# Samples' inputs and spread decays: the order of two TensorE blocks in a state-space stage

## The chip, the core and the metric

The kernel runs on one core of a Trainium2 chip. The metric is the device time of one execution in microseconds; the median of three runs of the kernel before is 1073.29 (1071.87 to 1075.68). TensorE does the matmuls and the transposes, VectorE and ScalarE the work between them, GpSimd issues the stores and SyncE most loads. Each engine runs its own list of instructions in order, and the lists meet at semaphores.

## What is computed

One inference step of two layers for a prompt of 256 tokens and for 8 samples with 4 new tokens each (32 sample tokens). Layer 0 is a short convolution beside block-sparse attention, layer 1 a Mamba-2 mixer, and each is followed by a SwiGLU network. The change lies in the mixer of layer 1, in the part for the samples. Cut to what matters there:

```
xbc = silu(causal_dwconv(xbc, conv_hist, conv_w) + conv_b)
xs, b_in, c_in = split(xbc)                    # 2048 inputs, 4 groups x 128 of B and of C
dt = softplus(dt + dt_bias);  a = -exp(a_log)
xdt = xs * dt
a_cum = cumsum(dt * a)
chunk_states = einsum('bclgn,bclgr,bclgrp->bcgrpn', b_in, exp(a_cum[-1] - a_cum), xdt)
state = state * exp(a_cum[-1]) + chunk_states  # one state of 32 heads x 64 x 128 a sample
y_diag = einsum(C B^T, exp(a_cum[l] - a_cum[s]), xdt);  y_off = einsum(C, old state, exp(a_cum))
```

So each of the 8 samples' states (1 MB each) is loaded, multiplied by a decay for each head, added to a product of weighed inputs and B, and stored.

## The kernel before

Everything is float32. Activations stand with channels on the 128 partitions and the 288 tokens (256 prompt, 32 sample) along the row; `NP:NT` are the samples' columns. `XBC` holds the convolved channels: 16 tiles of inputs, then B and C. After the last projection of layer 1, TensorE's list is: turn the per-head quantities (L1272 to L1276, read by VectorE into `tc`) and B (L1278 to L1283), the products of C and B for four groups (L1284 to L1290), then the part that the change touches:

- Spreading the decays (L1296 to L1300): 32 heads, one small matmul each, which the trace shows as 64 instructions, nine columns wide: the eight samples' decays and the skip weight of each head, from `decin`, are put on the 64 partitions of the head. VectorE copies the result to `dec` (L2583).
- Turning the samples' inputs (L1301 to L1305): for each of `G` = 4 groups, `PG` = 4 transposes of 128x32 pieces of `XBC` into one bank, so that the 32 sample tokens stand on partitions.
- Spreading the samples' sums for the differences (L1306 to L1312): 2 banks of 16 heads each, 64 matmul instructions in the trace.

Then `turn_state(0, q)` turns the four quarters of sample 0's state (L1315 to L1326), and the loop over the samples runs (L1371 to L1379): `new_state` multiplies weighed inputs `XW3` by B for one quarter (L1328 to L1339), `turn_state` turns a quarter of the next sample's state, `from_state` multiplies the old state by C (L1341 to L1349).

What orders this work: there are four banks `acc`, used in turn. `acc_open()` on TensorE (L831 to L836) waits until the bank four uses back was given free, and VectorE's `take()` (L1935 to L1940) waits for the bank next in the same count. So VectorE must read the banks in the order in which TensorE fills them, and a swap on one engine needs the same swap on the other.

VectorE's list there: the masked products of C and B (L2578 to L2582), the copy to `dec` (L2583), then for each group two products of the turned inputs with per-head weights, `XWT` (L2602) and `XDS` (L2603), and one group later the rest `XW3` (L2595, `rest_x`). Then the differences are added into `SEGS` (L2609), cut at zero (L2612), and the states are updated, 16 instructions a sample (L2620), each with a column of `dec`. Before each `rest_x`, ScalarE rounds that group's inputs twice (L1854, L1855). After the fourth group it makes a mask (L1836, `mask_b(1)`) and only then copies the turned quarters of state 0 (L1846). The third `turn_state` waits for the first of these copies (L1322). After its four quarters, a state is stored by GpSimd (L802 to L805); five states lie in a ring of buffers from before, one in a buffer of its own, and the last two are loaded by SyncE (L622 to L634) when the stores of states 0 and 1 have landed.

Of the kernel before, what the change touches and what calls it, by code (L numbers as in the profile page):

```python
# [23 lines left out]
P = 128  # L24
# [3 lines left out]
def hybrid_decoder_kernel(  # L28
# [8 lines left out]
):  # L37

    _, NP, D = x_prompt.shape
    NB, T, _ = x_sample.shape  # L40
    NS = NB * T
    NT = NP + NS
# [13 lines left out]
    CX = DI // P  # L56
    NST = state_ssm.shape[3]
    CC = state_conv_ssm.shape[2] // P
    G = (CC - CX) // 2
    HG = SH // G  # L60
    PG = HG // 2
# [32 lines left out]

    HIST_POS = 4
    Z_UNITS = [pos for pos, (kind, _) in enumerate(IN1) if kind == "z"]
    in1_units = [x for kind, i in IN1 for x in column_units(l1_w_in, (DI if kind == "c" else 0) + i * UC, 1)]

# [16 lines left out]
    with ExitStack() as ctx:  # L115
        def sb(name, shape, dt=F32):
            return ctx.enter_context(nc.sbuf_tensor(name, shape, dt))

        def sem(name):
            return ctx.enter_context(nc.semaphore(name))  # L120
# [109 lines left out]
        XBC = a.take(CC, NT)  # L230
# [35 lines left out]
        ident = sb("ident", [P, P])  # L266
# [30 lines left out]
        dec = a.take(CX, NB + 1)  # L297
# [55 lines left out]
        acc_full = sem("acc_full")  # L353
# [158 lines left out]
        def acc_bank(n):  # L512
            return acc[(n if n < ACC_MIX else n + 2) % 4]
# [92 lines left out]
        for w in (l0_norm_mix_pre, l0_norm_mix_post, l0_norm_ffn_pre, l0_norm_ffn_post,  # L606
                  l1_norm_mix_pre, l1_norm_mix_post, l1_norm_ffn_pre, l1_norm_ffn_post, l1_norm_gate):
            k = w.shape[0] // P
# [77 lines left out]
        def _(pool):  # L686
# [95 lines left out]
            for i, (src, _) in enumerate(conv_units):  # L782
                if i:
                    pool.wait_ge(cw_lo, 2 * i)
                pool.dma_start(WST, src).then_inc(cw_in, 16)
# [39 lines left out]
        def _(pe):  # L825
# [5 lines left out]
            def acc_open():  # L831
                n = n_acc[0]
                n_acc[0] += 1
                if n >= 4:
                    pe.wait_ge(acc_free, n - 3)
                return acc_bank(n)  # L836

            def tr_open(n):
                if n >= 2:
                    pe.wait_ge(tr_act if n % 2 == 0 else tr_dve, n // 2)  # L840
                return trb[n % 2]
# [137 lines left out]
            for k in range(KD):  # L979
                bank = tr_open(TR_X + k)  # L980
                for t in range(3):
                    rows = P if t < 2 else NS
                    last = pe.transpose(bank[:, t * P:t * P + rows], XIN[0:rows, t, k * P:(k + 1) * P], ident[0:rows, 0:rows])
# [26 lines left out]
            for i, m in enumerate((MK, MV)):  # L1010
                for t in range(3):
                    rows = P if t < 2 else NS
                    bank = tr_open(TR_KV + 3 * i + t)
                    for c in range(H * DH // P):
                        last = pe.transpose(bank[0:rows, c * P:(c + 1) * P], BIG[:, m + c, t * P:t * P + rows], ident[:, :])
# [243 lines left out]
            bank = acc_open()  # L1259
            pe.wait_ge(wdt_lo, 2)  # L1260
            for k in range(KD):
# [3 lines left out]
                last = pe.matmul(bank[0:SH, 0:NT], low, HX1[:, k, 0, :], start=False, stop=(k == KD - 1))  # L1265
# [6 lines left out]
            bank = acc_open()  # L1272
            for t in range(3):
                rows = P if t < 2 else NS
                last = pe.transpose(bank[0:rows, t * P:(t + 1) * P], hs[:, t * P:t * P + rows], ident[:, :])
            last.then_inc(acc_full, 1)  # L1276
            pe.wait_ge(xc_made, 2 * CC)
            for t in range(3):  # L1278
                rows = P if t < 2 else NS
                bank = acc_open()  # L1280
                for g in range(G):
                    last = pe.transpose(bank[0:rows, g * NST:(g + 1) * NST], XBC[:, CX + g, t * P:t * P + rows], ident[:, :])
                last.then_inc(acc_full, 1)  # L1283
            for g in range(G):  # L1284
                bank = acc_open()
                for t in range(3):
                    rows = P if t < 2 else NS
                    cols = slice(t * P, t * P + rows)
                    last = pe.matmul(bank[0:rows, cols], XBC[:, CX + g, cols], XBC[:, CX + G + g, cols], start=True, stop=True)
                last.then_inc(acc_full, 1)  # L1290
            def spread_head(out, h, of_heads):

                half = slice(h % 2 * DH, (h % 2 + 1) * DH)
                return pe.matmul(out[half, :], ident[0:SH, h:h + 1].to_broadcast([SH, DH]), of_heads, start=True, stop=True)

            bank = acc_open()  # L1296
            for h in range(SH):
                k = h // 2
                last = spread_head(bank[:, k * (NB + 1):(k + 1) * (NB + 1)], h, decin[:, :])
            last.then_inc(acc_full, 1)  # L1300
            for g in range(G):  # L1301
                bank = acc_open()
                for c in range(PG):
                    last = pe.transpose(bank[0:NS, c * P:(c + 1) * P], XBC[:, g * PG + c, NP:NT], ident[:, :])
                last.then_inc(acc_full, 1)  # L1305
            for i in range(2):  # L1306
                bank = acc_open()
                for hh in range(SH // 2):
                    h = i * SH // 2 + hh
                    last = pe.matmul(bank[0:NS, hh * NS:(hh + 1) * NS], ident[0:SH, h:h + 1].to_broadcast([SH, NS]), hw[:, 0, NP:NT],  # L1310
                                     start=True, stop=True)
# [148 lines left out]
            for g in range(G):  # L1460
# [10 lines left out]
                for c in range(PG):  # L1471
                    bank = acc_open()
                    for r in range(2):
# [3 lines left out]
                        for t in range(2):  # L1477
                            pe.matmul(bank[rows, t * P:(t + 1) * P], XDT[:, gp, t, cols], SEG[gp][:, hh, t * P:(t + 1) * P],
                                      start=True, stop=(t == 0))
                        last = pe.matmul(bank[rows, P:2 * P], SENT[gp][:, cols], CE[gp][hh // 4][:, hh % 4 * P:(hh % 4 + 1) * P],  # L1480
                                         start=False, stop=True)
# [12 lines left out]
            for i in range(2):  # L1494
                pe.wait_ge(x_made, 3 * KD + 4 * i + 4)
                for t in range(3):
                    rows = P if t < 2 else NS
                    for c in range(4):
                        last = pe.transpose(Y_BANKS[3 * i + t][0:rows, c * P:(c + 1) * P], X[:, 4 * i + c, t * P:t * P + rows], ident[:, :])
# [432 lines left out]
        def _(dve):  # L1932
            n_acc, chain, n_r = [0], [0], [0]

            def take():  # L1935

                n = n_acc[0]
                n_acc[0] += 1
                dve.wait_ge(acc_full, n + 1)
                return acc_bank(n)  # L1940

            def free(ins):
                ins.then_inc(acc_free, 1)
# [74 lines left out]
            for i, m in enumerate(range(MQ, M_IN0)):  # L2018
                bank = take()
# [20 lines left out]
            for r in range(2):  # L2040
                rows = slice(r * DH, (r + 1) * DH)
                last = dve.tensor_copy(KNZ[rows, :, :].rearrange("p (c r) n -> p c r n", r=2)[:, :, r, :],
                                       BIG[rows, MK:MK + H // 2, NP:NT])
# [519 lines left out]
            bank = take()  # L2563
# [14 lines left out]
            for g in range(G):  # L2578
                bank = take()
                dve.tensor_tensor(CBM[:, g, 0:NP].rearrange("p (t c) -> p t c", c=P), bank[:, 0:NP].rearrange("p (t c) -> p t c", c=P),  # L2580
                                  trilT[:, :].unsqueeze(1).to_broadcast([P, 2, P]), ALU.mult)
                free(dve.tensor_tensor(CBM[0:NS, g, NP:NT], bank[0:NS, NP:NT], bd01[:, :], ALU.mult))  # L2582
            free(dve.tensor_copy(dec[:, :, :], take()[:, 0:CX * (NB + 1)].rearrange("p (k c) -> p k c", c=NB + 1)))  # L2583

            def by_head(rows, t, first, g):

# [5 lines left out]
            def rest_x(g):  # L2592
                cols = slice(g * HG * DH, (g + 1) * HG * DH)
                dve.wait_ge(xw_hi, 2 * g + 2)
                dve.tensor_tensor(XW3[2 * NS:S3, cols], XWT[g % 2][0:NS, :], XW3[0:NS, cols], ALU.subtract).then_inc(xw_lo, 1)  # L2595

            for g in range(G):
                bank = take()
# [5 lines left out]
                if g >= 1:  # L2604
                    rest_x(g - 1)
            rest_x(G - 1)
            for i in range(2):
                mine = slice(i * SH // 2, (i + 1) * SH // 2)
                free(dve.tensor_tensor(SEGS[0:NS, mine, :], take()[0:NS, :].rearrange("p (h n) -> p h n", n=NS),  # L2609
                                       tc[0:NS, 2, AC + i * SH // 2:AC + (i + 1) * SH // 2].unsqueeze(2).to_broadcast([NS, SH // 2, NS]), ALU.add))  # L2610
# [3 lines left out]
            for b in range(NB):  # L2614
                st = state_home(b)[0]
                for q in range(G):
                    bank = take()
                    for hh in range(PG):
                        k = q * PG + hh
                        last = dve.scalar_tensor_tensor(st[:, k, :], st[:, k, :], dec[:, k, b:b + 1],  # L2620
                                                        bank[:, hh * NST:(hh + 1) * NST], ALU.mult, ALU.add)
# [59 lines left out]
            for g in range(G):  # L2681
# [9 lines left out]
                for c in range(PG):  # L2691
                    k = g * PG + c
# [46 lines left out]
```

## Time and profile before

| | us |
|---|---|
| median of three runs | 1073.29 (1071.87 to 1075.68) |
| the profiled execution | 1074.21 |
| its span, first to last instruction | 1072.5 |
| TensorE busy with matmuls | 1022.2 (95%) |
| VectorE busy | 691.8 (65%) |
| ScalarE busy | 500.0 (47%) |

A busy time is a sum over the whole span; what a change in one stage can do is read from the order of events in that stage. The instruments are the chain of work that ended last, which follows from the end back to what released each step; the timeline of one engine, with the idle time before an instruction and its releaser; and the stretches, which give each engine's busy time and the clock granted to TensorE (1.00 is 2.4 GHz, 0.50 is 1.2 GHz). Times in the trace count from the start of the span.

### The profile page before, as it was taken

How to read it: one execution, taken by the hardware profiler on the slowest of the kernel's cores; microseconds unless marked ns; L12 is line 12 of the kernel's file. 1: busy time of each engine (PE TensorE's matmuls, PEld its weight loads, DVE VectorE, ACT ScalarE, POOL GpSimd, SP SyncE). 2: the span in 40 equal slices, each digit the busy share in tenths (PEclk: the TensorE clock that was granted, in tenths of full speed). 3: DMA queues.
4: the chain of work that ended last, by engine and by line, in shares of the span. 5: the costliest groups of instructions: out<-in, count | busy, mean ns of one | idle time of the engine just before them, and what ended most of it. 6: DMA issues, size and time to landing. Idle time of an engine off the chain costs nothing.

```text
span 1072.5 us, 22412 instructions
## 1 busy us (share of the span) xinstructions
PE 1022.2 (95%) x9097; PEld 941.6 (88%) x9097; DVE 691.8 (65%) x1284; ACT 500.0 (47%) x899; POOL 56.4 (5%) x106
## 2 busy tenths in 40 slices
PE   9999999997899999999999999899899899999996
PEld 8987886664789999999889999678789799999996
DVE  5556787544467656634588996788965766665343
ACT  5233453421454334434457764565754544444331
POOL 6050000000000000000000000021000000000000
PEclk8999999998899999999999999699999999999999
DMA  9859999999935555445335565098145255544501
GB/s 302 232 153 349 348 347 346 348 348 347 296 91 184 158 163 178 151 156 178 120 118 158 173 180 145 15 295 318 31 140 175 80 167 181 164 157 144 181 31 45
DMA packets 187782, 206.22 MB, mean 192 GB/s; under 512 B 7226, under 2 KB 178447, under 8 KB 187628
## 3 DMA queue, kind: packets, MB, share of 16 engines
q1 hardware_dynamic: 166222, 170.79, 50.6%
q0 software_dynamic: 5680, 18.79, 5.4%
q10 hardware_dynamic: 15776, 15.21, 4.5%
q8 instruction: 72, 1.18, 0.5%
q14 instruction: 32, 0.25, 0.1%
HBM read 192.59 MB, written 12.17 MB: 191 GB/s over the span
## 4 chain that ended last, share of the span: by engine, by line
PE 73%; DVE 9%; SPq 8%; DMA 5%; issue 2%; ACT 1%; ACTq 0%; POOL 0%; DVEq 0%
PE acc L935 20%; PE acc L937 20%; PE acc L936 19%; SPq L658 8%; DMA ring<-in_cache_k_dram 2%; PE scb L1180 2%; DVE X L2402 1%; DMA ring<-in_state_ssm_dram 1%; DVE Y L2399 1%; DVE HX L1979 1%; PE trb L1030 1%; PE acc L1163 1%; DMA ring<-in_cache_v_dram 1%; DMA out_dram<-ring 1%; PE scb L1051 1%
## 5 line engine op out<-in xcount | busy, mean ns | idle before, releaser
L935 PE MATMUL acc<-HX,WHL 128*128 128x288 f32 x800 | 238.2, 298 | 3.0 <-DVE HX L1977 1.3
L936 PE MATMUL acc<-HX,WHL 128*128 128x288 f32 x800 | 236.0, 295 | 0.0
L937 PE MATMUL acc<-HX,WHL 128*128 128x288 f32 x800 | 235.8, 295 | 0.0
L1545 ACT ACTIVATE WHL<-ring 128x1024 fp32r<-128x1024 f32 x126 | 124.7, 1038 | 165.5 <-PE acc L937 160.2
L1990 DVE TENSOR_TENSOR WHL<-ring,WHL 128x1024 fp32r<-128x1024 f32 x126 | 146.9, 1206 | 62.4 <-ACT WHL L1545 62.3
L935 PEld LDWEIGHTS acc<-HX,WHL 128*128 128x128 f32 x800 | 150.6, 188 | 4.8 <-DVE ext L2446 1.5
L936 PEld LDWEIGHTS acc<-HX,WHL 128*128 128x128 f32 x800 | 151.8, 190 | 0.0
L937 PEld LDWEIGHTS acc<-HX,WHL 128*128 128x128 f32 x800 | 151.6, 189 | 0.0
L1545 ACT ACTIVATE W<-ring 128x1024 fp32r<-128x1024 f32 x84 | 82.6, 1031 | 132.6 <-PE acc L937 129.9
L1990 DVE TENSOR_TENSOR W<-ring,W 128x1024 fp32r<-128x1024 f32 x84 | 97.1, 1197 | 52.8 <-ACT W L1545 52.7
L935 PE MATMUL acc<-HX,W 128*128 128x288 f32 x336 | 99.5, 296 | 0.2 <-DVE Z L2416 0.2
L936 PE MATMUL acc<-HX,W 128*128 128x288 f32 x336 | 98.8, 294 | 0.0
L937 PE MATMUL acc<-HX,W 128*128 128x288 f32 x336 | 98.7, 294 | 0.0
L936 PEld LDWEIGHTS acc<-HX,W 128*128 128x128 f32 x336 | 63.5, 189 | 0.0
L935 PEld LDWEIGHTS acc<-HX,W 128*128 128x128 f32 x336 | 63.0, 187 | 0.6 <-DVE Z L2416 0.4
L937 PEld LDWEIGHTS acc<-HX,W 128*128 128x128 f32 x336 | 63.4, 189 | 0.0
L935 PE MATMUL acc<-HID,W 128*128 128x288 f32 x176 | 52.1, 296 | 0.0
L935 PE MATMUL acc<-HID,WHL 128*128 128x288 f32 x176 | 52.1, 296 | 0.0
L936 PE MATMUL acc<-HID,WHL 128*128 128x288 f32 x176 | 51.7, 294 | 0.0
L936 PE MATMUL acc<-HID,W 128*128 128x288 f32 x176 | 51.7, 294 | 0.0
L937 PE MATMUL acc<-HID,W 128*128 128x288 f32 x176 | 51.7, 294 | 0.0
L937 PE MATMUL acc<-HID,WHL 128*128 128x288 f32 x176 | 51.7, 294 | 0.0
(447 smaller groups left out, 2053.6 us busy)
## 6 DMA issues: line engine op xcount, KB each, us to landing
ring<-in_l_w_in_dram SPq DMA_DIRECT2D x26, 1024.0 KB, 5.3
ring<-in_l_ffn_gate_dram SPq DMA_DIRECT2D x22, 1024.0 KB, 5.3
ring<-in_l_ffn_up_dram SPq DMA_DIRECT2D x22, 1024.0 KB, 5.3
ring<-in_cache_k_dram SPq DMA_DIRECT2D x83, 256.0 KB, 7.2
ring<-in_cache_v_dram SPq DMA_DIRECT2D x76, 256.0 KB, 7.8
ring<-in_l_ffn_down_dram SPq DMA_DIRECT2D x16, 1024.0 KB, 5.1
ring<-in_l_w_out_dram SPq DMA_DIRECT2D x11, 1024.0 KB, 9.7
ring<-in_cache_v_dram ACTq DMA_DIRECT2D x32, 256.0 KB, 7.5
```

The source lines that it names most:

```text
L658: sp.dma_start(dst, src).then_inc(landed, 16)
L935: pe.matmul(out, w[:, 0, at:at + P], part_at(k, 0), start=(k == 0), stop=False)
L936: pe.matmul(out, w[:, 0, at:at + P], part_at(k, 1), start=False, stop=False)
L937: last = pe.matmul(out, w[:, 1, at:at + P], part_at(k, 0), start=False, stop=(k == kdim - 1))
L1030: last = pe.transpose(TURNED[q][jp][:, hh * P:(hh + 1) * P], keys[:, 4 * q + hh, 2 * jp:2 * jp + 2, :].rearrange("p j d -> p (j d)"), iden ...
L1051: last = pe.matmul(scb[e][g * QT:(g + 1) * QT, s * P:(s + 1) * P], QZ[:, e, q, hh * QT:(hh + 1) * QT], KTB[p % 2][:, jp, q, hh * P:(hh + 1 ...
L1163: pe.matmul(bank[:, 0:NT], w[:, 0, at], HX0[:, k, 0, :], start=(k == 0), stop=False)
L1180: last = pe.matmul(bank[j * QT:(j + 1) * QT, :], S[:, b, s, j * QT:(j + 1) * QT], POOL[(N_SLOT + b * KVS + s) % NPL][:, :, j, :], start=(s ...
L1545: act.activation(split_weights(i)[:, 0, half], source[:, half], ACT.Copy).then_inc(w_hi, 1)
L1979: ins = dve.scalar_tensor_tensor(hx[:, k, 1, :], X[:, k, :], par[:, 0, col:col + 1], hx[:, k, 0, :], ALU.mult, ALU.subtract)
L1990: dve.tensor_tensor(w[:, 1, half], landing(i)[0][:, half], w[:, 0, half], ALU.subtract).then_inc(w_lo, 1)
L2399: link(dve.tensor_tensor(y, y, SPREAD_R.unsqueeze(1).to_broadcast([P, size, NT]), ALU.mult))
```

## The change

TensorE turns the samples' inputs first and spreads the decays after them. VectorE reads the banks in the new order: the copy to `dec` moves from ahead of the products of the inputs to behind the last of them and its rest, ahead of `SEGS`. No instruction is added, removed or altered.

```diff
@@ -1293,16 +1293,16 @@
+            for g in range(G):
+                bank = acc_open()
+                for c in range(PG):
+                    last = pe.transpose(bank[0:NS, c * P:(c + 1) * P], XBC[:, g * PG + c, NP:NT], ident[:, :])
+                last.then_inc(acc_full, 1)
             bank = acc_open()
             for h in range(SH):
                 k = h // 2
                 last = spread_head(bank[:, k * (NB + 1):(k + 1) * (NB + 1)], h, decin[:, :])
             last.then_inc(acc_full, 1)
-            for g in range(G):
-                bank = acc_open()
-                for c in range(PG):
-                    last = pe.transpose(bank[0:NS, c * P:(c + 1) * P], XBC[:, g * PG + c, NP:NT], ident[:, :])
-                last.then_inc(acc_full, 1)
@@ -2580,7 +2580,6 @@
-            free(dve.tensor_copy(dec[:, :, :], take()[:, 0:CX * (NB + 1)].rearrange("p (k c) -> p k c", c=NB + 1)))
@@ -2604,6 +2603,7 @@
                 if g >= 1:
                     rest_x(g - 1)
             rest_x(G - 1)
+            free(dve.tensor_copy(dec[:, :, :], take()[:, 0:CX * (NB + 1)].rearrange("p (k c) -> p k c", c=NB + 1)))
```

## Rows read from the trace of the kernel before

**Rows 1.** The page: granted clock in 40 slices, and the chain's shares by engine.

```profile
PEclk8999999998899999999999999699999999999999
...
PE 73%; DVE 9%; SPq 8%; DMA 5%; issue 2%; ACT 1%; ACTq 0%; POOL 0%; DVEq 0%
```

**Rows 2.** The chain that ended last, 672 to 722: start, duration, engine, tile, line.

```profile
672.17 3.34 PE acc L1294 x64
...
676.51 0.68 DVE hists L2602
...
683.92 0.72 ACT BM L1836
...
687.95 0.87 PE trb L1324 x4
...
693.28 2.17 DVE ring L2620 x8
...
701.86 7.38 DMA out_dram<-ring
...
709.30 12.00 DMA ring<-in_state_ssm_dram
...
721.35 0.66 PE trb L1324 x4
```

**Rows 3.** Timeline of TensorE: start, duration, instruction, count, idle before and releaser.

```profile
675.44 3.59 PE L1304 MATMUL acc<-ident,Z 128*32 128x128 f32 x16
678.96 2.35 PE L1310 MATMUL acc<-Z,ident 32*32 32x32 f32 x64
681.24 1.09 PE L1324 MATMUL trb<-ident,ring 128*128 128x128 f32 x8
685.26 1.94 PE L1324 MATMUL trb<-ident,ring 128*128 128x128 f32 x8 [2.93 <-ACT Z L1846]
```

**Rows 4.** Timeline of VectorE, 673 to 688.

```profile
673.23 0.17 DVE L2582 TENSOR_TENSOR Z<-acc,bd 32x32 f32<-32x32 f32 x1
675.55 0.31 DVE L2583 COPY late<-acc 128x144 f32<-128x144 f32 x1 [2.15 <-PE acc L1294]
...
682.50 0.67 DVE L2603 TENSOR_TENSOR Z<-acc,late 32x512 f32<-32x512 f32 x1
...
683.92 0.68 DVE L2595 TENSOR_TENSOR XW<-ext,XW 32x512 fp32r<-32x512 f32 x1
...
687.99 1.12 DVE L2620 SCALAR_TENSOR_TENSOR ring<-ring,late,acc 128x128 f32<-128x128 f32 x4 [1.36 <-PE acc L1337]
```

**Rows 5.** Stretches: length, busy by engine (count), granted clock, DMA share, GB/s.

```profile
672.60:675.40 2.80, 2.80 (x56) 2.80 (x54) 0.80 (x4) 0.00 (x0) 0.00 (x0) 0.50 0.01 4
675.50:678.90 3.40, 3.40 (x17) 2.16 (x16) 2.70 (x5) 1.63 (x3) 0.00 (x0) 0.50 0.00 0
679.50:681.20 1.70, 1.70 (x58) 1.70 (x54) 1.56 (x4) 1.65 (x4) 0.00 (x0) 1.00 0.05 14
...
685.30:689.50 4.20, 4.20 (x21) 4.20 (x22) 2.42 (x7) 3.13 (x5) 0.00 (x0) 0.50 0.00 0
689.60:692.80 3.20, 3.20 (x15) 1.21 (x14) 1.12 (x4) 1.56 (x3) 0.00 (x0) 0.50 0.00 0
...
700.00:720.00 20.00, 20.00 (x176) 15.93 (x175) 17.44 (x66) 13.65 (x25) 4.64 (x4) 1.00 0.93 292
```

**Rows 6.** The chain again, later, where the clock is granted in full.

```profile
722.40 0.46 PE trb L1324 x4
...
738.99 1.98 PE acc L1294 x64
```

**Rows 7.** Timeline of ScalarE: the third copy of a turned quarter.

```profile
686.39 0.60 ACT L1846 ACTIVATE Z<-trb 128x512 f32<-128x512 f32 x1 [0.79 <-PE trb L1324]
```

**Rows 8.** Timeline of GpSimd: the first store of a state.

```profile
696.36 1.21 POOL L768 DMA_DIRECT2D out_dram<-ring  x1 [28.61 <-DVEq L2624]
```

**Rows 9.** Waits of SyncE's queue, 690 to 760: total, times, longest.

```profile
SPq L634 <- DMA out_dram<-ring: 69.6, 7, 35.9
```

## The prediction

> **What bounds the kernel now.** I read the page first. The granted clock and the shares of the chain that ended last [rows 1] say that TensorE carries the program as a whole: 73% of the chain is its own work, and the rest is short stretches in which it waits for somebody. The change touches one of these stretches, some 20 us long, between the last projection of layer 1 and the recurrent states. So the question is which piece ends last there, and the chain of work in order of time answers it [rows 2]. Read it downward. From 672.17 the chain is TensorE spreading the decays (64 small matmuls, 3.34 us), then the first four transposes of the samples' inputs, and at 676.51 VectorE takes over with its weighing of these inputs. VectorE stays the chain until ScalarE rounds the last group and makes a mask (683.92, 0.72 us). ScalarE can copy the first turned state only then, at 684.64. TensorE, whose own list had been done long before, goes on at 685.26 [rows 3]. From there TensorE feeds VectorE, which updates states 0 and 1; the store of state 1 (7.38 us) and the load of the last state into the same buffer (12.00 us) bring the chain to 721.35.
>
> The timeline of each engine says who waits. On TensorE [rows 3] the spread, the transposes, the samples' differences and two turned states follow each other without a hole from 672.17 to 682.33, and then it waits 2.93 us for ScalarE's copy. On VectorE [rows 4] the last masked product starts at 673.23 and takes 0.17; then VectorE waits 2.15 us for the spread, copies it in 0.31, waits again (0.65 us) for the first transposes, and has no hole more until its first state update at 687.99, before which it waits 1.36 us.
>
> **The change, part by part.** It adds and removes nothing. It swaps two blocks in TensorE's list and moves one VectorE copy behind the eight products and four remainders of the inputs. No DMA is issued in the moved pieces and no other engine's list changes, so SyncE's and GpSimd's queues are passed by nothing.
>
> (1) TensorE starts the transposes at 672.17 in place of the spread. Their first bank opens with the same release as the spread's did, so the start is the same. The first group took 1.07 us from its start at 675.44 to VectorE's product at 676.51 [rows 3, 2], so it would be ready at 673.24. VectorE is busy until 673.23 + 0.17 = 673.40 [rows 4]. It therefore ends last by 0.16 us, and its first product starts near 673.45 instead of 676.51. That is 3.06 us earlier. The following groups need four transposes each 0.9 us (3.52 us for sixteen, from 675.44 to 678.96 [rows 3]), against 1.2 us of VectorE's products a group, so TensorE stays ahead. Their banks open with the releases of the masked products, all done by 673.40.
>
> (2) VectorE and ScalarE run the same lists against each other as before, 3.06 us earlier. ScalarE's mask, which ended at 684.64 [rows 2], ends at 681.58.
>
> (3) The copy of the turned state needs TensorE as well, and TensorE's list is now the new thing that could be late. It does the same three blocks before it turns a state. The transposes end at 672.17 + 3.52 = 675.7. The spread costs 3.34 us where the granted clock is 0.50, the 1.2 GHz level [rows 2, 5]. The trace has no spread of nine columns at 2.4 GHz; the nearest row is the same instruction with 32 columns, 64 of them in 1.98 us, granted 1.00 there [rows 6]. So the spread is between 1.98 and 3.34. The 64 matmuls of the differences took from 678.96 to 681.24, 2.28 us, nearly all at the high level [rows 3, 5]; at the low level I estimate 64 x 3.34 / 64 = 3.3 us, since they are of the same kind and number as the spread. Which level? Before, the clock stood at the low level through the spread and the transposes and was at the high one from 679.5, after TensorE had done 3.5 us of nothing but these transposes [rows 5]. With the transposes first, I expect the rise after them, near 675.9, so the spread at the high level (675.7 to 677.8), and a fall again after these small matmuls, as before (1.00 from 679.5 to 681.2, 0.50 at 685.3 [rows 5]), which may make the last third of the differences slow: 677.8 + 2.28 + 0.4 = 680.4. Turned states would then be ready 1.1 us after that (as from TensorE's start at 685.26 to ScalarE's copy at 686.39, at the low level [rows 3, 7]), at 681.5, level with ScalarE's 681.58. The copy starts at about 681.6 against 684.64: 3.0 us gained.
>
> The Trainium skill, TensorE: Matmul & The Clock Gate, Part 4: PE-mode transpose, speaks against this: a transpose does not count as activity for the clock gate the way a matmul does, so the full clock does not engage for it. By that rule putting the transposes first leaves the spread and the differences at 1.2 GHz. The trace does not bear it out, for the rise before 679.5 followed nothing but these transposes [rows 5]; the result by the rule is the second rival below.
>
> (4) The copy of the spread decays, 0.31 us, was hidden in a wait of VectorE; it now stands between the last remainder (683.92 + 0.68 before [rows 4], so it ends at 681.54) and the state differences. The spread is there by 677.8, or 679.1 at the low level, so VectorE waits for nothing. What hides the 0.31 is VectorE's 1.36 us of waiting before its first update [rows 4]; if that cover is gone it costs 0.31. The banks of the differences and of the first new state now open with the second products of groups 1 to 3; the last of them, 682.50 + 0.67 before [rows 4], now ends at 680.1 and the two others some 2.1 and 4.2 us sooner, each ahead of TensorE; at no cost, and at most some 0.3 us if TensorE should be faster than I say.
>
> (5) From the copy on, the work is the old one: 685.26 to 693.28, 8.0 us, all at 0.50 [rows 2, 5]. The two moved parts do not touch it, but its price hangs on the clock: four turned blocks cost 0.87 there and 0.46 at the full clock [rows 2, 6]. TensorE will no longer stand idle for the 2.9 us ahead of it. In the forecast the low level stays for this stretch.
>
> (6) What is late next? Both successors move along. The stores wait for VectorE (the first is issued at 696.36, right after its updates [rows 8]), the loads for the stores, 69.6 us of such waiting [rows 9], and the DMA engines are idle until then (share 0.00 from 685.3 to 692.8 [rows 5]). The load is waited for at 721.35 [rows 2]; both it and TensorE's list ahead of it hang on the same first copy. After that the chain is TensorE, ScalarE and VectorE again, so a shift survives to the end.
>
> The sum against the profiled execution: its span is 1072.5 us [rows 1] and its time 1074.21. With 3.0 gained, 1071.2. But this execution lies 0.9 above the median of 1073.29, and its spread ran wholly at the low clock. Had it run at the high level, the old start of VectorE's products would be 3.34 - 1.98 = 1.4 us earlier and the transposes some 0.4 us quicker, while the new start is set by VectorE's 673.40 whatever the clock; the gain would be 1.3. Between 3.0 and 1.3 I take 2.5, nearer to what is shown: 1073.29 - 2.5 = 1070.8.
>
> **The rivals.** First, the clock comes back early. TensorE's hole of 2.93 us goes, and if the stretch of (5) runs at 2.4 GHz its pieces shrink to about half; ScalarE's copies and its exponential then bound it, and I make the first state done some 2.5 us sooner still: gain 3.2 to 5.5, about 1069.0. For it: busier TensorE. Against: 685.3 to 689.5 was busy without a hole and still at 0.50 [rows 5].
>
> Second, TensorE becomes the late one. If spread and differences both stay at the low level, it turns the first state from 675.7 + 3.34 + 3.3 = 682.3, the copy starts 1.1 us later at 683.4, and the gain is 1.2 or less, 1072.1 and up. For it: the low clock at 672.6, with the same two kinds of work close by; against: the rise before 679.5 [rows 5].
>
> Third, the change is hidden anyway: the load of the last state, in the chain with 12.00 us [rows 2], would come no sooner. For it: the DMA engines' share was 0.93 between 700 and 720 [rows 5]. Against: it is work that itself starts with the stores, so I give this little: 1073.3.
>
> Fourth, slower. The low clock holds on into the state loop. There TensorE's blocks cost 0.87 against 0.46 [rows 2, 6], so each microsecond of low clock loses about 0.47. To eat the 3.0 of the gain and 3.2 more, the low level must last 6.2 / 0.47 = 13 us beyond the shifted 690, to 703: then 1076.5. For it: TensorE's mix of dense and tiny pieces shifts against the clock's steps. Against: in the same loop the clock stood at 1.00 between 700 and 720 [rows 5].
>
> **How the numbers follow.** Forecast (gain 1.9 to 3.2) 0.52; clock early 0.2; TensorE late (gain 0.5 to 1.9) 0.19; hidden 0.05; slower 0.04. What a measurement of this kernel can tell from no change is about 0.3%, 3.2 us. Above it lie the clock rival and 0.1 of the forecast's chance: faster 0.3. Slower by more than that is the fourth rival with a little for its neighbours: 0.05. The rest, 0.65, is within 0.3%. The range leaves out the far end of the first rival and the slower cases: 1067.8 to 1072.9.
>
> **What would show it.** In the profile of the changed kernel: VectorE's first product near 673.45 with no wait for the spread behind it; ScalarE's first copy near 681.6; TensorE's hole before the third turned block of the first state under 1 us; the granted clock at 1.00 somewhere between 676 and 679; the first store near 693.3 instead of 696.36; the last state's load 3 us earlier. It is wrong if the first copy starts after 683, if the decays' copy waits for TensorE, or if the clock stays at 0.50 past 693.

## The result, and the profile after

The changed kernel takes 1070.78 us (median of 20 runs, 1065.84 to 1074.68), the kernel before 1074.01 (20 runs, 1070.86 to 1079.82). The ratio is 0.9965, with a 95% interval of 0.9951 to 0.9979. The gain is therefore 2.3 to 5.3 us, the difference of the medians 3.2. The profiled execution took 1071.70 us with a span of 1070.0; the one of before had 1074.21 and 1072.5.

In the kernel after, L1299 is the transposes of the samples' inputs (L1304 before), L2601, L2602 and L2594 are the two products and the rest (L2602, L2603 and L2595 before), and L2606 is the copy of the decays (L2583 before). L1294 is still the spread and L1310 the differences. First the page: the clock in 40 slices and the chain's shares, to be read beside [rows 1].

```profile
PEclk9999999998899999999999999899999999999999
...
PE 77%; DVE 10%; SPq 6%; DMA 4%; issue 1%; ACT 1%; ACTq 0%; POOL 0%; DVEq 0%
```

The slice that was a 6 before is an 8; the chain's shares by engine moved by up to 4 points, over the whole span, and say little of a change of 3 us. The chain that ended last, from the masked products on, answers to [rows 2]:

```profile
673.58 0.33 DVE Z L2580
673.91 0.10 DVE Z L2582
674.01 0.60 DVE hists L2601
...
681.34 0.72 ACT BM L1836
...
682.68 1.94 PE trb L1324 x8
...
690.70 2.17 DVE ring L2620 x8
...
699.27 7.20 DMA out_dram<-ring
...
706.54 12.27 DMA ring<-in_state_ssm_dram
...
718.86 0.66 PE trb L1324 x4
```

No TensorE step stands between the last masked product and the first product of the inputs: VectorE goes straight on. The spread (3.34 us before) is out of the chain. The rest is the same chain, with durations within 0.3 us of the old ones. TensorE's timeline, beside [rows 3]:

```profile
672.78 1.92 PE L1299 MATMUL acc<-ident,Z 128*32 128x128 f32 x16 [1.12 <-DVE Z L2582]
675.26 2.03 PE L1294 MATMUL acc<-decin,ident 32*64 32x9 f32 x64 [0.56 <-DVE Z L2602]
677.22 2.52 PE L1310 MATMUL acc<-Z,ident 32*32 32x32 f32 x64
679.68 1.57 PE L1324 MATMUL trb<-ident,ring 128*128 128x128 f32 x8
682.68 1.94 PE L1324 MATMUL trb<-ident,ring 128*128 128x128 f32 x8 [1.44 <-ACT Z L1846]
```

The sixteen transposes take 1.92 us and not 3.59, so TensorE even has to wait 0.56 us for the bank of the spread, which opens only with VectorE's second product of the first group. Its hole ahead of the third turned quarter is 1.44 us in place of 2.93. VectorE and ScalarE, beside [rows 4] and [rows 7]:

```profile
673.84 0.17 DVE L2582 TENSOR_TENSOR Z<-acc,bd 32x32 f32<-32x32 f32 x1
673.94 0.67 DVE L2601 TENSOR_TENSOR hists<-acc,late 32x512 f32<-32x512 f32 x1
...
682.06 0.31 DVE L2606 COPY late<-acc 128x144 f32<-128x144 f32 x1
682.28 1.27 DVE L2609 TENSOR_TENSOR Z<-acc,late 32x512 f32<-32x512 f32 x2
...
685.41 1.12 DVE L2620 SCALAR_TENSOR_TENSOR ring<-ring,late,acc 128x128 f32<-128x128 f32 x4 [1.14 <-PE acc L1337]
```

```profile
681.97 1.06 ACT L1846 ACTIVATE Z<-trb 128x512 f32<-128x512 f32 x2
```

VectorE's two waits (2.15 and 0.65 us) are gone, the decays' copy has no wait ahead of it, and the cover ahead of the first update shrank from 1.36 to 1.14. Then the stretches, beside [rows 5], and the first store, beside [rows 8]:

```profile
672.80:674.70 1.90, 1.90 (x16) 1.25 (x16) 1.90 (x8) 0.06 (x1) 0.00 (x0) 1.00 0.03 9
675.30:680.00 4.70, 4.57 (x131) 4.39 (x132) 4.43 (x8) 3.81 (x6) 0.00 (x0) 1.00 0.02 5
680.30:690.20 9.90, 8.46 (x40) 6.09 (x38) 6.08 (x15) 7.17 (x11) 0.00 (x0) 0.50 0.00 0
690.50:700.00 9.50, 9.50 (x86) 7.57 (x85) 9.01 (x31) 6.95 (x12) 1.95 (x2) 1.00 0.38 111
```

```profile
693.77 1.22 POOL L768 DMA_DIRECT2D out_dram<-ring  x1 [25.42 <-DVEq L2624]
```

The clock stood at the low level once, some 10 us long, where before it did so twice, some 7 and 10 us.

The work ahead of the stage shifts by some microseconds from execution to execution: the first masked product (L2580) starts at 671.61 before and at 672.21 after. So I count every time in this stage from the start of that product, in all kernels. These differences of timeline starts are the measure that the experiments rest on:

| kernel | first product of inputs | first copy of a quarter | first store | end of the span | clock low in the stage, us | clock low 50 to 150 us on |
|---|---|---|---|---|---|---|
| before | 4.90 | 12.93 | 24.75 | 400.9 | 6.8 and 10.2 | never |
| before, again | 4.70 | 12.73 | 25.24 | 401.6 | 6.8 and 13.7 | 3.4 |
| after | 1.73 | 9.76 | 21.56 | 397.8 | 10.2 | never |
| after, again | 1.73 | 10.01 | 20.18 | 398.0 | 10.2 | 3.4 |

In the profiled pair the change gains 3.17 us at the first product, 3.17 at the first copy and 3.19 at the first store (the load's end at 721.35 and 718.86 makes 3.09), and the span falls by 2.5, since the stage began 0.6 later. From the first masked product to the end of the span it is 3.1, and 3.6 in the second pair, so the gain lasts to the end.

### The profile page after: what moved, and what is told of

Read it like the earlier page. It is cut to its first block, busy times and chain, and to the rows that moved or that the text cites. A ratio compares the mean times of both kernels' runs of the same rounds, so it can differ in the third digit from the quotient of the medians.

```text
span 1070.0 us, 22412 instructions
## 1 busy us (share of the span) xinstructions
PE 1019.9 (95%) x9097; PEld 940.8 (88%) x9097; DVE 691.9 (65%) x1284; ACT 500.2 (47%) x899; POOL 60.7 (6%) x106
## 4 chain that ended last, share of the span: by engine, by line
PE 77%; DVE 10%; SPq 6%; DMA 4%; issue 1%; ACT 1%; ACTq 0%; POOL 0%; DVEq 0%
PE acc L935 20%; PE acc L937 20%; PE acc L936 19%; SPq L658 5%; PE trb L1030 2%; PE scb L1051 2%; PE acc L1030 2%; PE scb L1180 2%; DMA ring<-in_cache_k_dram 1%; DVE X L2402 1%; DMA ring<-in_state_ssm_dram 1%; DVE Y L2399 1%; DVE HX L1979 1%; DVE WHL L1990 1%; PE acc L1163 1%
```

## The experiments

Two theories. A: VectorE waited for the spread, and the change takes it out of VectorE's way; the clock sets only the price. B: the order is worth little, and the difference came from the clock that the executions happened to get. All ratios are to the kernel before, with their 95% interval; the kernel before had medians of 1073.87, 1074.35 and 1074.86 us beside the three sets.

**The two kernels once more.**

> The changed kernel once more, for a second execution's trace: where the clock's steps fall in it, and whether VectorE's first product of the inputs starts right behind the last masked product (within 0.1 us) at whatever level the transposes run. Theory A: yes, and the distance from the first masked product to the first update of a state stays at 12.9 us within some tenths. Theory B: the distance changes with the level by 1 us or more.

> The kernel before once more, for another trace of it. Theory A: VectorE waits for the spread whatever the clock; with the spread at 2.4 GHz its first product of the inputs comes 3.2 us behind the first masked product, at 1.2 GHz 4.9, and the distance to the first store is 22.4 to 24.8, never the changed kernel's 20.2 to 21.6 unless the low stretch is shorter too.

After, again: 1070.04 us, ratio 0.9964 (0.9935 to 0.9993). Before, again: 1073.44, ratio 0.9994 (0.9974 to 1.0013). The table has their distances. The first store of before, again, at 25.24, is later than the 24.8 I had allowed, with a low stretch of 13.7 us. The first product of the inputs starts at 1.73 in both executions of the changed kernel. The second, with the lines of its TensorE and then of its chain, shows the rival in which TensorE is late, at a small price:

```profile
671.27 1.92 PE L1299 MATMUL acc<-ident,Z 128*32 128x128 f32 x16 [1.11 <-DVE Z L2582]
673.75 2.33 PE L1294 MATMUL acc<-decin,ident 32*64 32x9 f32 x64 [0.56 <-DVE Z L2602]
676.01 3.62 PE L1310 MATMUL acc<-Z,ident 32*32 32x32 f32 x64
679.55 3.83 PE L1324 MATMUL trb<-ident,ring 128*128 128x128 f32 x16
```

```profile
673.10 0.61 DVE Z L2602
...
673.75 2.33 PE acc L1294 x64
676.08 3.55 PE acc L1310 x64
679.62 3.77 PE trb L1324 x16
```

The clock fell at 675.3, the differences cost 3.62 us at the low level, TensorE has no hole behind the spread, and the first copy comes at 10.01 instead of 9.76. Here the chain runs through TensorE from its wait for the spread's bank on. The clock also came back 3.3 us sooner, counted in the stage (at 14.8, against 18.2), and the store is 1.4 us sooner although the copy was 0.25 later: 1.63 / 3.3 = 0.49 us for each microsecond of low clock in the state loop, an estimate from one pair of traces, where the prediction had 0.47. At the end of the span nothing of the sooner store is left (398.0 against 397.8), in an execution whose clock fell once more, for 3.4 us from 729.9. In the second trace of before, both the spread and the transposes ran at the low level again:

```profile
673.70:680.30 6.60, 6.60 (x77) 5.28 (x76) 3.95 (x9) 2.44 (x4) 0.00 (x0) 0.50 0.01 2
```

**The spread twice, in either kernel.** The same edit in both:

```diff
-            for h in range(SH):
+            for h in [*range(SH), *range(SH)]:
                 k = h // 2
                 last = spread_head(bank[:, k * (NB + 1):(k + 1) * (NB + 1)], h, decin[:, :])
```

> The kernel before, with the 64 spreading matmuls issued twice into the same bank. Theory A (the spread stands whole on the path of the kernel before, since VectorE waits for it): everything behind moves by one more spread, +2.0 us where it runs at 2.4 GHz and +3.3 us at 1.2 GHz; VectorE's wait ahead of its copy of the decays grows by the same. Theory B (the gain of the change came from the clock that its execution happened to get, and the order is worth little): also about +2 here; this run alone does not tell them apart, it gives the price beside which the next one is read.

> The changed kernel with the same doubled spread. Theory A: the spread is now off the path, and TensorE's hole of 1.44 us ahead of the third turned block takes part of the second spread; what is over delays the first copy of a turned state: 2.0 - 1.4 = +0.6 us at 2.4 GHz, 3.3 - 1.4 = +1.9 at 1.2 GHz, VectorE's first product of the inputs not moved at all against its masked products. Theory B: the order is worth little, so the doubled spread costs here what it costs in the kernel before, +2.0 or more.

Before with it: 1081.25 us, ratio 1.0065 (1.0042 to 1.0087). After with it: 1071.09, ratio 0.9975 (0.9960 to 0.9989), 0.3 us above the changed kernel's median. The same doubled work costs about 7 us in one order and is lost in the noise in the other. VectorE's rows say why, first of the kernel before with the doubled spread, then of the changed one:

```profile
679.77 0.31 DVE L2583 COPY late<-acc 128x144 f32<-128x144 f32 x1 [5.34 <-PE acc L1294]
680.73 0.68 DVE L2602 TENSOR_TENSOR hists<-acc,late 32x512 f32<-32x512 f32 x1 [0.65 <-PE acc L1304]
```

```profile
672.63 0.17 DVE L2582 TENSOR_TENSOR Z<-acc,bd 32x32 f32<-32x32 f32 x1
672.73 0.67 DVE L2601 TENSOR_TENSOR hists<-acc,late 32x512 f32<-32x512 f32 x1
...
680.85 0.31 DVE L2606 COPY late<-acc 128x144 f32<-128x144 f32 x1
```

In the old order VectorE's wait grew from 2.15 to 5.34 us, and the first copy moved by 3.21 us, to 16.14. In the new order VectorE notices nothing up to its copy of the decays. TensorE does: spread and differences cost 5.50 and 3.62 us there, mostly at the low level, and the first copy comes at 13.18, 3.4 us later; more than the 0.6 to 1.9 that I had expected, because I had not reckoned with slow differences in that run. But its first store is only 0.7 later (22.30), with the clock back at 15.1, and the end of its span 0.8 later (398.6). Theory B's +2 us or more for the changed kernel is not there in the medians; by the intervals it cannot be excluded by the times alone, but VectorE's untouched start can't come from it.

The 7 us are more than the added spread. The trace gives +3.21 at the first copy, +3.9 at the first store and +8.2 at the end of the span (409.1). The clock was low for 10.2 and 13.7 us in the stage, and it fell twice more, further on, for 3.4 us each:

```profile
741.00:747.00 6.00, 6.00 (x61) 4.85 (x59) 4.95 (x6) 1.19 (x2) 0.00 (x0) 0.72 1.04 383
789.00:794.00 5.00, 4.21 (x20) 4.24 (x21) 4.73 (x12) 4.67 (x10) 0.00 (x0) 0.66 0.61 210
```

At 0.49 us for each microsecond these two falls make an estimated 3.3 of the further 4.3 us. The first trace of before had no such fall, the second had one (3.4 us from 779.4), so that they follow from the delay is not shown.

**The spread elsewhere.** One kernel takes it ahead of the products of C and B, the other between the second and third group of inputs, with VectorE's copy moved alike:

```diff
+            bank = acc_open()
+            for h in range(SH):
+                k = h // 2
...
             for g in range(G):
                 bank = acc_open()
                 for t in range(3):
```

```diff
             for g in range(G):
+                if g == 2:
+                    bank = acc_open()
+                    for h in range(SH):
...
                 bank = acc_open()
                 for c in range(PG):
```

> The kernel before, with the spread (and VectorE's copy of it) moved the other way: ahead of the products of C and B. Theory A: what counts is only that VectorE does not wait for the spread between its masked products and its products of the inputs. TensorE has 1.1 us of hole there and its products are ahead of VectorE, so nearly the whole gain appears here too: the first product of the inputs within 0.1 us behind the last masked product or some 0.7 us later, 2.1 to 2.8 us earlier than in the kernel before; time -2 to -3 against the kernel before. Rival: only transposes first keeps the clock up; then nothing like it here, 0 to -1.

> The spread (and VectorE's copy of the decays) between the second and the third group of inputs, half of the change. Theory A (it matters only that VectorE has work while TensorE spreads): the first product of the inputs starts 1.7 us behind the first masked product, as in the changed kernel; the third group waits at most 0.5 us; VectorE's copy of 0.31 us is now ahead of the last groups, so the first copy of a turned quarter comes at 10.1 to 10.5 instead of 9.8; the gain is 2.5 to 3 us of the change's 3. Rival (all transposes must come first): half of the gain.

The first: 1071.19 us, ratio 0.9982 (0.9961 to 1.0002); first product at 1.97, first copy at 10.00, first store at 20.15. The second: 1071.59, ratio 0.9973 (0.9953 to 0.9992); 1.73, 9.90 and 21.69, a little better than the 10.1 to 10.5 I had expected at the copy. At the first copy both have over nine tenths of the change's 3.17 us (2.93 and 3.03). The times do not separate either of them from the changed kernel. So the transposes need not all come first; it is enough that VectorE does not stand at the spread. These two do not separate that from the clock, for in both the spread took 2.03 us and the transposes ran at the high level (in the first TensorE has no hole at this place at all).

**How much of it is the clock.** Nine dummy transposes, one behind the other, fill TensorE's hole ahead of the stage; in the changed kernel six more fill the hole ahead of the third turned quarter:

```diff
+            def filler(count):
+                pe.wait_ge(r_read, n_spread[0])
+                for _ in range(count):
+                    pe.transpose(scb[1][:, 0:P], ident[:, :], ident[:, :])
+
+            filler(9)
             bank = acc_open()
             for h in range(SH):
```

> The kernel before, with nine dense dummy transposes in TensorE's hole of 1.1 us ahead of the spread. Theory A with the clock as the second term: the spread runs more often at 2.4 GHz, so VectorE's products start up to 1.4 us sooner against the masked products, -0.5 to -1.4 us; the change's own 3 us are not reached. Theory B (the clock is the whole gain): -3 us, as the change.

> The changed kernel, with the same nine dummies ahead of the transposes and six more in its hole ahead of the third turned quarter. Theory A: VectorE's start does not hang on the clock any more, so the first nine gain nothing; the six may let the clock come back sooner than 10 us after its fall, at most 4 us of gain if the low stretch between 680 and 690 disappears, and 0 if the level does not answer to them. Theory B: -1 to -2 from the first nine alone.

Before with the filler: 1071.48 us, ratio 0.9970 (0.9948 to 0.9991), a gain of 1.0 to 5.6 us, at its middle more than the 0.5 to 1.4 that theory A gave it. Its TensorE (L1310 is the transposes there, L1330 a turned state) and VectorE (L2608 is the first product):

```profile
673.31 2.03 PE L1294 MATMUL acc<-decin,ident 32*64 32x9 f32 x64
675.28 1.92 PE L1310 MATMUL acc<-ident,Z 128*32 128x128 f32 x16
...
679.58 1.09 PE L1330 MATMUL trb<-ident,ring 128*128 128x128 f32 x8
```

```profile
675.93 0.68 DVE L2608 TENSOR_TENSOR hists<-acc,late 32x512 f32<-32x512 f32 x1 [0.23 <-PE acc L1310]
```

The spread cost 2.03 us and each block of the transposes shrank too, so the first product starts at 3.18, the first copy at 11.22, the first store at 22.40, the end of the span at 398.5, with the clock low for 10.2 us once. This splits the change: of 3.17 us at the first copy, 12.93 - 11.22 = 1.71 can be had by keeping the clock, and 11.22 - 9.76 = 1.46 only by the order. So theory A holds, but the clock is a good half of what it explains, and not as B had it: the clock was low under nearly all of the spread and the transposes in all three traces of the old order without a filler, and under the transposes in none of the new one, so it went with the order and not with the execution. The split rests on one trace of each kernel; by their times the filler in the old order and the reordering cannot be told apart. The changed kernel with fillers: 1070.74, ratio 0.9958 (0.9939 to 0.9977). As expected the first nine moved nothing (1.73 and 9.76); the low stretch was 6.8 us and the first store at 19.67. Whether that came from the six is not shown, since kernels without fillers had 6.8 us too.

**What ends last behind the change.** ScalarE's second mask moved behind its second copy:

```diff
-            mask_b(1)
             for b in range(NB):
                 for q in range(G):
                     copy_state(b, q)
+                    if (b, q) == (0, 1):
+                        mask_b(1)
```

> The changed kernel, with ScalarE's second mask moved behind its second copy of a turned quarter, where it waits 0.78 us for TensorE anyway. If ScalarE's list ends last ahead of the first copy, as the chain of the changed kernel says, the first copy starts 0.63 us sooner (some 9.3 us behind the end of the first masked product in place of 9.4 + 0.5) and all behind it moves by 0.6, -0.6 us in time, less than the comparison can tell. If TensorE's turned state ends last, nothing moves.

1069.83 us, ratio 0.9957 (0.9941 to 0.9973). The first copy starts at 9.12, 0.64 us sooner, as it must if ScalarE's list ends last; the first update too (12.59 against 13.20). The store is at 21.66, with a low stretch of 13.6 us. The time does not separate it from the changed kernel.

ScalarE's first two copies ahead of its last rounding, and its second mask behind the third copy (cut to the copies):

```diff
             for g in range(G):
+                if g == G - 1:
+                    copy_state(0, 0)
+                    copy_state(0, 1)
                 cols = slice(g * HG * DH, (g + 1) * HG * DH)
```

> The changed kernel, with ScalarE's first two copies of turned quarters ahead of its rounding of the last group of inputs, and the second mask behind the third copy. ScalarE idles 0.82 us there and the first quarter is turned by then. Expected: TensorE's hole of 1.44 us shrinks to nothing and the third turned quarter starts 1.4 us sooner; VectorE's last rest waits 1.7 us for the rounding, which eats VectorE's 1.14 us of waiting ahead of its first update and 0.6 more; net -0.5 to -1.4 us up to the first store. Rival: VectorE is the next bound, the rounding is on its path, and the whole comes out at 0 or +0.6.

1071.38 us, ratio 0.9962 (0.9942 to 0.9983). It failed in its mechanism: the clock fell at 4.8 in the stage, the differences were slow, and the first copy came at 9.84, no sooner, while VectorE had to wait for the rounding (first update at 15.34 instead of 13.20). The row of the copy names TensorE:

```profile
683.05 0.60 ACT L1846 ACTIVATE Z<-trb 128x512 f32<-128x512 f32 x1 [2.84 <-PE trb L1324]
```

So I put the first two turned quarters ahead of the differences, one copy into ScalarE's hole, the second behind the rounding, and the second mask behind the third; and the same with nine and four dummies (cut to TensorE's list):

```diff
             for q in range(G):
                 turn_state(0, q)
+                if q == 1:
+                    for i in range(2):
+                        bank = acc_open()
...
```

> The changed kernel, with two more moves: TensorE turns the first two quarters of state 0 ahead of the samples' differences, and ScalarE copies the first quarter in its hole of 0.8 us ahead of the last rounding, the second behind it, its second mask behind the third. Counted from the first masked product, the first copy goes from 9.8 us to 7.0, the third turned quarter starts with TensorE's list at 8.3 instead of 10.5, and VectorE (free at 12.0) is then the bound of its first update, 12.1 instead of 13.2. Theory A (the path runs through these lists): the first store 1.1 to 1.7 us sooner than in the changed kernel at the same steps of the clock, about -4.5 us against the kernel before. Rival (the clock decides, the lists do not matter): the first store moves only with the length of the low stretch, 20 to 21.5 us, as in the changed kernel's two executions.

> The same with nine dense dummy transposes ahead of the inputs' and four ahead of the third turned quarter. If density brings the clock back sooner, its low stretch is 6.8 us, as with the fillers alone, and not 10.2, and the first store another 1.5 us sooner; about -5.5 against the kernel before. If the level does not answer to them, the same as the kernel without them, or some tenths later.

Without dummies: 1071.56 us, ratio 0.9968 (0.9952 to 0.9984). With them: 1068.79 (7 runs), ratio 0.9941 (0.9920 to 0.9962), the lowest of all, 0.6% below the kernel before; its interval still overlaps that of the changed kernel, so it is not shown to beat that. The first copy comes at 7.0 in both, as planned, but the third quarter no sooner. TensorE of the one without dummies (L1317 is the turned quarters, L1368 the differences):

```profile
673.36 1.97 PE L1317 MATMUL trb<-ident,ring 128*128 128x128 f32 x8
675.25 3.62 PE L1368 MATMUL acc<-Z,ident 32*32 32x32 f32 x64
678.80 1.97 PE L1317 MATMUL trb<-ident,ring 128*128 128x128 f32 x8
```

The differences at the low level take 3.62 us and end where ScalarE's copy had ended before: one list took the other's place. The first update came at 13.36, where I had expected 12.1. With this low stretch 13.7 us long the first store was at 21.77, with dummies (10.2 us, where I had hoped for 6.8) at 20.66. And neither store tells of the end: in both traces the end of the span, counted as in the table, is at 401.9, as late as in the kernel before, after two more falls of the clock, 6.8 and 3.4 us long. The first of them, without dummies:

```profile
727.00:735.00 8.00, 8.00 (x77) 6.74 (x73) 5.31 (x6) 0.96 (x2) 0.68 (x2) 0.57 1.04 379
```

At 0.49 us for each microsecond such falls cost an estimated 5 us. What brought them is not shown, so the lowest median has no trace that explains it.

## Why the prediction was right, and where it was not

The forecast was 1070.8 us and the measured median is 1070.78. Part of that closeness is luck, point by point:

(1) The start of VectorE's products. Forecast 3.06 us earlier, measured 3.17; the product overlaps the last masked product (673.84 and 673.94), so no gap stood there. It held in every kernel with the new order, always 1.73.

(2) and (3) The copy starts 3.0 us sooner: measured 3.17 and 2.92. ScalarE's list ended last in the first trace, TensorE's in the second, by 0.15 us. The reason I gave for a fast spread was wrong: I let the clock fall at the start of the stage, as before, and rise after the transposes. It did not fall there at all (1.00 from 672.8 to 674.7). In all seven traces that start the stage with transposes and have nothing in the hole ahead of it, it fell 4.6 to 7.9 us into the stage, when the transposes were over and small matmuls had begun. Two prices were off as well. The differences at the low level take 3.62 us, not 3.3; and I gave the spread no wait for its bank, which costs TensorE 0.56 us and is on the chain of the second trace. So TensorE's hole was 1.44 us in the first trace, not under 1 as I had said. My reading that the rise before 679.5 followed nothing but transposes was also a little too strong: it came at 679.3, 0.4 us into the differences, and 0.8 us into them in the other two traces of the old order, with a single spread ahead of the transposes or a double one.

The Trainium skill, TensorE: Matmul & The Clock Gate, Part 4: PE-mode transpose, says that the full clock does not engage for transposes and that they do not count as busy in the same way; these runs do not agree, for behind the same hole of 1.1 us the clock fell 0.9 to 1.2 us into the stage in all three traces that go on with nine-column matmuls, and in none of those seven before their transposes were over.

(4) The decays' copy of 0.31 us: hidden, with no wait ahead of it; the wait that covers it fell from 1.36 to 1.14 us. Right.

(5) The stretch behind the copy kept its price (8.0 us from 682.68 to 690.70, as from 685.26). Right in the first trace; in the second it was shorter.

(6) The shift survives the transfers: 7.20 and 12.27 us against 7.38 and 12.00. Right. In the second trace of before, the load is not in the chain but TensorE's own list is, so there it had landed before it was needed, and hid nothing.

The sum is the mis-sized step. I lowered 3.0 to 2.5 because an execution of before might have its spread at 2.4 GHz, and took that off a median of three runs, 1073.29. None of the three traces of the old order without a filler showed such a spread, and the median of more runs is 1074.01. For a spread at the high level the filler gives the gain as 1.46 us, near the 1.3 I had worked out; it is the weight given to that case that was wrong. The measured gain is 3.2 us by the medians and 3.8 by the ratio, so the two errors, 0.7 in the base and 0.7 in the gain, cancelled in the time. They did not cancel in the chances: I gave 0.3 to faster by over 0.3% and 0.65 to no more than that, while the ratio stands at -0.35%, with an interval from -0.21% to -0.49%, on the edge of the two.

Of the rivals, an early clock (gain 3.2 to 5.5) describes the second trace of the changed kernel up to the first store, 4.6 us against the first trace of before, but only 2.9 are left at the end of the span; TensorE being late showed with 0.25 us; the hidden and the slower one did not show.

## What to carry to other kernels

When one engine fills buffers that another must empty in the same order, put first what the reader can start on, and put the small matmuls, whose result is wanted late, behind it. Read the gain from the reader's start: it is the end of the reader's own work that sets it then. And price each block at both levels of the clock, for a reordering also changes which block stands there when TensorE comes out of a hole. Count to the end of the span as well as to the next event: a gain at the first store can be gone by then.

## What I had not expected of the hardware

TensorE can be busy and lose its clock: from 675.30 to 680.00 it was busy for 4.57 of 4.70 us, with matmuls of 9 and 32 columns, and the level went from 1.00 to 0.50 at 680.1. Such matmuls pay less than double for it: 64 of nine columns cost 2.03 us at the high level and 3.34 at the low one, 64 of 32 columns 2.39 and 3.62, where the sixteen transposes cost 1.92 and 3.59. And the low stretch has been 6.8, 10.2 or 13.7 us long for nearly the same work, which alone moves the first store by an estimated 1.7 us either way; that is half of the change, and no single trace shows it. The same holds for the falls further on, which were absent in some executions and 10.2 us long in others.
